# Two SSD heads in turn on the two column halves, and gate squares summed in full precision

## The reference

```python
y_diag = jnp.einsum('bgcls,bghcls,bcsghp->bclghp', cb, Lmat, xc)        # inside a chunk of 128 tokens
...
y_off = jnp.einsum('bclgn,bcghpn,bghcl->bclghp', Cc, states, jnp.exp(a_cum))   # from the chunks before
...
y = y_fwd + y_bwd + xs * d_skip.reshape(SSM_GROUPS, SSM_HEADS_PER_GROUP)[..., None]
y = y.reshape(b, S, SSM_W) * jax.nn.silu(z)
y = rms_norm(y.reshape(b, S, SSM_GROUPS, SSM_W // SSM_GROUPS),
             norm_g.reshape(SSM_GROUPS, SSM_W // SSM_GROUPS))
```

## Time and profile before

| | us |
|---|---|
| median of 3 runs (1583.84 to 1584.5) | 1584.28 |
| the profiled execution | 1584.14 |
| its span, first to last instruction | 1582.4 |
| PE busy in it | 1554.7 |
| DVE busy | 944.8 |
| ACT busy | 733.8 |

### The profile page before, as it was taken

How to read it: one execution, slowest core, us unless ns; L and a number is a source line. 1 busy time by engine, 2 the same in 40 slices (tenths; PEclk the granted TensorE clock), 3 DMA queues, 4 the chain that set the end, 5 groups by cost and what they waited for, 6 DMA issues and landing times.

```text
span 1582.4 us, 25561 instructions
## 1 busy us (share of the span) xinstructions
PE 1554.7 (98%) x9693; PEld 1395.8 (88%) x9693; DVE 944.8 (60%) x1226; ACT 733.8 (46%) x1011; POOL 35.0 (2%) x36
## 2 busy tenths in 40 slices
PE   6999999999999999999999999999999999999998
PEld 6999999998888888888889998899988998889987
DVE  5878787778666666665465554364454455435543
ACT  4476556656354544444443443434433344424431
POOL 0000000000100000000000000000000000000000
PEclk9999999999999999999999999999999999999999
DMA  8776666555566656575656655666555665666564
GB/s 233 227 216 175 184 174 174 172 175 154 161 186 175 180 176 178 175 237 180 195 181 182 185 183 192 193 166 183 190 190 171 186 181 192 191 174 183 186 196 136
DMA packets 186324, 291.50 MB, mean 184 GB/s; under 512 B 13533, under 2 KB 67151, under 8 KB 185984
## 3 DMA queue, kind: packets, MB, share of 16 engines
q1 hardware_dynamic: 183748, 285.92, 60.3%
q10 hardware_dynamic: 2492, 4.36, 0.9%
HBM read 288.04 MB, written 5.34 MB: 185 GB/s over the span
## 4 chain that ended last, share of the span: by engine, by line
PE 95%; DMA 2%; DVE 1%; ACT 1%; issue 0%; DVEq 0%; SPq 0%; ACTq 0%
PE psum L1178 94%; DMA raw<-in_w_in 1%; DVE w_lo L776 1%; DMA x_in<-in_x 1%; PE psum L1288 0%; PE psum L1308 0%; PE psum L1221 0%; DMA decay_rows<-prefix 0%; PE psum L1231 0%; ACT w_hi L478 0%; DVE xg L751 0%; ACT mix L507 0%; ACT squares_act L464 0%; DVE actT_lo L771 0%; SPq L298 0%
## 5 line engine op out<-in xcount | busy, mean ns | idle before, releaser
L776 DVE TENSOR_TENSOR w_lo<-raw,w_hi 128x1024 fp32r<-128x1024 f32 x512 | 611.0, 1221 | 165.4 <-ACT w_hi L478 162.0
L478 ACT ACTIVATE w_hi<-raw 128x1024 fp32r<-128x1024 f32 x512 | 527.8, 1053 | 390.0 <-DMA raw<-in_w_down 166.2
L1178 PE MATMUL psum<-actT_lo,w_hi 128*128 128x256 f32 x1792 | 514.1, 287 | 9.6 <-DVE w_lo L776 9.6
L1178 PE MATMUL psum<-actT_hi,w_hi 128*128 128x256 f32 x1792 | 509.5, 284 | 0.0
L1178 PE MATMUL psum<-actT_hi,w_lo 128*128 128x256 f32 x1792 | 509.4, 284 | 0.0
L1178 PEld LDWEIGHTS psum<-actT_lo,w_hi 128*128 128x128 f32 x1792 | 346.3, 193 | 14.4 <-DVE w_lo L776 9.4
L1178 PEld LDWEIGHTS psum<-actT_hi,w_lo 128*128 128x128 f32 x1792 | 346.3, 193 | 0.2
L1178 PEld LDWEIGHTS psum<-actT_hi,w_hi 128*128 128x128 f32 x1792 | 346.3, 193 | 0.0
L1178 PE MATMUL psum<-w_hi,hid_lo 128*128 128x512 f32 x512 | 199.2, 389 | 0.0
L1178 PE MATMUL psum<-w_lo,hid_hi 128*128 128x512 f32 x512 | 199.2, 389 | 0.0
L1178 PE MATMUL psum<-w_hi,hid_hi 128*128 128x512 f32 x512 | 199.2, 389 | 0.0
(11 more groups left out here) (192 smaller groups left out, 1277.7 us busy)
## 6 DMA issues: line engine op xcount, KB each, us to landing
raw<-in_w_in SPq DMA_DIRECT2D x128, 512.0 KB
raw<-in_w_up SPq DMA_DIRECT2D x128, 512.0 KB
raw<-in_w_down SPq DMA_DIRECT2D x128, 512.0 KB
raw<-in_w_out SPq DMA_DIRECT2D x64, 512.0 KB
raw<-in_w_in SPq DMA_DIRECT2D x64, 256.0 KB
raw<-in_w_in SPq DMA_DIRECT2D x128, 128.0 KB
decay<-decay_rows SPq DMA_DIRECT2D x16, 512.0 KB, 5.5
rel_tiles<-rel_rows ACTq DMA_DIRECT2D x1, 3072.0 KB, 19.8
```

What stands on the lines that cost most here:

```text
L478: act.activation(w_hi[j][:, :, :], raw[j][:, :, :], ACT.Copy).then_inc(hi_ready, 1)
L776: tt_(w_lo[j][:, :, :], raw[j][:, :, :], w_hi[j][:, :, :].bitcast(f32), ALU.subtract).then_inc(lo_dve, 1)
L1178: return pe.matmul(o, lhsT, rhs, start=first, stop=last, **kw)
```

## The change

It has three parts. The four products of two heads are issued in turn: first product of the even head, first of the odd one, then the second of each, and so on. The squares of the gate are summed as they are by fp32 matmuls with one moving column; the rounded copy, the low part, their tiles and their semaphores go. And the two loads of decay rows in a window are issued at slots 4 and 16 instead of 2 and 14.

```diff
@@ SP, decay_loads
-                if s == 2 and m is not None:
+                if s == 4 and m is not None:
                     sp.wait_ge(decays_ready, 8 * m + 4)
                     load_decay(2 * m + 1)
-                if s == 14 and m is not None and w is not None:
+                if s == 16 and m is not None and w is not None:
                     sp.wait_ge(decays_ready, 8 * w)
                     load_decay(2 * w)
@@ ACT, ssd_slot
                         act.activation(gate_sq[:, :, :], gate[:, :, :], ACT.Square).then_inc(gate_squared, 1)
-                        act.wait_ge(gate_squared, G + 1)
-                        act.activation(sq_hi[:, :, :], gate_sq[:, :, :], ACT.Copy).then_inc(sq_high, 1)
@@ DVE, ssd_slot
-                    if k == 9:
-                        dve.wait_ge(sq_high, G + 1)
-                        tt_(sq_lo[:, :, :], gate_sq[:, :, :], sq_hi[:, :, :].bitcast(f32), ALU.subtract)\
-                            .then_inc(sq_low, 1)
@@ PE, ssd_slot
                     if k in (5, 7):
                         pe.wait_ge(xtok_ready, G + 1)
                         pe.wait_ge(mix_ready, 4 * G + k - 3)
-                        for h in (k - 5, k - 4):
-                            rows, ch = slice(64 * (h % 2), 64 * (h % 2) + 64), slice(64 * h, 64 * h + 64)
-                            c0 = SEQ * (h // 2)
-                            both, second, first = slice(c0, c0 + SEQ), slice(c0 + P, c0 + SEQ), slice(c0, c0 + P)
-                            mm(M0[rows, both], xdt_f[:, 0, ch], mix[h][:, 4:6, :], True, False)
-                            mm(M0[rows, both], xdt_b[:, 1, ch], mix[h][:, 0:2, :], False, False)
-                            mm(M0[rows, second], xdt_f[:, 1, ch], mix[h][:, 2, :], False, False)
-                            mm(M0[rows, first], xdt_b[:, 0, ch], mix[h][:, 3, :], False, True).then_inc(y_done, 1)
+
+                        for n, (xdt, t, blocks, c0, c1) in enumerate((
+                                (xdt_f, 0, slice(4, 6), 0, SEQ), (xdt_b, 1, slice(0, 2), 0, SEQ),
+                                (xdt_f, 1, slice(2, 3), P, SEQ), (xdt_b, 0, slice(3, 4), 0, P))):
+                            for h in (k - 5, k - 4):
+                                base = SEQ * (h // 2)
+                                ins = mm(M0[64 * (h % 2):64 * (h % 2) + 64, base + c0:base + c1],
+                                         xdt[:, t, 64 * h:64 * h + 64], mix[h][:, blocks, :], n == 0, n == 3)
+                                if n == 3:
+                                    ins.then_inc(y_done, 1)
                     if k == 10:
-                        pe.wait_ge(sq_low, G + 1)
-                        pe.wait_ge(ones_rounded, 1)
+                        pe.wait_ge(gate_squared, G + 1)
                         pe.wait_ge(cb_masked, G + 1)
                         for t in range(TT):
-                            for n, (sq, c) in enumerate(((sq_lo, 0), (sq_lo, 1), (sq_hi, 0), (sq_hi, 1))):
-                                ins = mm(M1[:, 2 * t:2 * t + 2], sq[:, c, P * t:P * t + P], ones_r[:, 0:2], n == 0, n == 3)
+                            for c in range(2):
+                                ins = mm(M1[:, 2 * t:2 * t + 1], gate_sq[:, c, P * t:P * t + P],
+                                         ones_r[:, 0:1].bitcast(f32), c == 0, c == 1)
                         ins.then_inc(norm_summed, 1)
```

More of the change, by code:

```diff
@@ L172, in build @@
         rnorm = place("rnorm", [P, SEQ], at=at_of(lo2, 1024))
-        sq_hi = place("sq_hi", [P, 2, SEQ], f32r, at=cat_base + 32768)
-        sq_lo = place("sq_lo", [P, 2, SEQ], f32r, at=at_of(lo2, 2048))
         norm_ms, norm_root = small[:, 32:34], small[:, 34:36]
@@ L240, in build @@
         x_in_s = [sem(f"x_in{t}") for t in range(TT)]
-        table_in, ones_rounded, sq_high, sq_low = (sem(n) for n in ("table_in", "ones_rounded", "sq_high", "sq_low"))
+        table_in, ones_rounded = sem("table_in"), sem("ones_rounded")
         rows_in, relw_in, col_in, dtw_in, dskip_in = (sem(n) for n in (
```

## The result

The changed kernel takes 1568.96 us in the median (four runs, 1568.2 to 1569.55) against 1584.06 for the kernel before: a ratio of 0.9904, with a 95% interval of 0.9887 to 0.9921. The forecast was 1569.0.

What follows compares the result with a forecast made beforehand. The prediction took PE (TensorE), busy 98% of the span, as the bound. 1584.14 - 14.6 (products) - 0.7 (clock) = 1568.8, other terms zero; the median lies 0.14 above, so 1569.0 us, range 1566 to 1573.5.

Steps and rivals of the forecast that it cites:

- The products: SSD products of two heads in turn: first to last start falls from 2.16 to 1.25 us, 14.6 us over 16 pairs.
- The look ahead: SSD products in PE's queue: PE passes over three unstarted records today, so it should pass over one in the new order.
- Rival 1: SSD products: starts follow the program order, 1.51 us a pair, gain only 10.4 us, 1573.2 us; chance 0.10.
- Rival 3: SSD products: alternation serialises the halves, 2.55 us a pair against 2.16, +6.2 us, 1589.8 us; chance 0.04.
- Rival 4: SSD products: the overlap is only how records are drawn, so the order is indifferent, 1584 us; chance 0.03.
- The sums: Sums of squares of the gate: eight records a group stay eight, about 0.1 us each, so zero.
- Neither bound: Sums of squares: -3.6 us if four records only, +0.8 us if a restart of 0.1 us at each group.
- The dropped operations: One ACT copy and one DVE subtraction a group: nobody on PE waits for them, so worth nothing.
- the decay loads: Two DMAs each issued two slots later on SP: weights are fetched with lead, so zero on PE.
- the link from sums to spread: PE, GpSimd, DVE, PE between sums and spread: lead of 0.38 us remains, costed at nothing.
- Rival 2: Spread: DVE and ACT fall behind in shorter windows, a new wait gives 7.2 us back, 1576 us; chance 0.05.
- The clock: Gaps between MLP quarters: one and a half lower-clock episodes instead of two, -0.7 us, between -3.0 and +1.5.

Runs made afterwards that it cites:

- turns of two and three: The changed kernel, but each head issues two, or three, products before the other has its turn: 1569.31 and 1576.67 us (one execution each).

## Why the prediction was right, and where it wasn't

**The products: right in mechanism and size.** 0.91 us a pair and 14.6 us were forecast; PE's records give 40.96 - 26.35 = 14.6. The step that carried it was the reading of the earlier trace rows, a start of the second head ahead of the first head's last records, with neither slower. The look ahead was sized from the same rows (over three records), and turns of two and three confirmed it; that it ends there could be read in the same timeline, where B stood still with four ahead. Rivals 1, 3 and 4 fell: 1.25 us a pair, not 1.51; 2.54 only where both heads share a half; and the order is not indifferent.

**The sums: right.** Zero was taken; 7.2 us of PE's program before and after, and a ratio of 1.000 for that part alone. Neither bound was needed.

**The dropped operations and the decay loads: zero was right for each alone, wrong beside the new order.** The prediction took the longest idle of SP to be without worth, since PE did not wait for weights, and looked at the link from sums to spread in one later group only. There the stretch isn't shortened, and the 0.38 us of lead did remain. In group 0, DVE was late in the kernel before already, and the lead there, 0.70 us, was spent by the 1.8 us by which the sums came sooner. Rival 2 had the mechanism; it struck in one group, not in eight, 1.3 us with the order alone, and the decay loads, costed at nothing, kept it away. Without them, but with the other two parts, it cost 0.7 us.

**The clock: mis-sized.** -0.7 us was taken for half an episode less. Both profiled executions had two, and over all profiles 27 of 36 gaps drew one, so 2.25 would have been the better guess than 1.5, and the term about zero (without it the forecast is 1569.7). The profiled executions differ by 1584.14 - 1569.34 = 14.8 us: 14.6 for the products and 0.2 for a shorter wait for the first conv output (0.5 and 0.3 us). So nothing stands for the 0.7 in the profiles. That the median came out at 1569.0 as forecast is in part luck: the single executions lie between 1568.2 and 1569.55, and a fourth one moved the median of the kernel before from 1584.28 to 1584.06.

## What to carry to other kernels

Where a matmul's output fills half the partitions, issue it in turn with one for the other half, with no more than three records between; look in the timeline for a start that comes ahead of program order, since it shows both that halves overlap and how far PE looks. When PE is the bound and a stretch of its program shrinks, check each link PE, VectorE, GpSimd, PE in the worst group, not in a typical one, and mind what stands ahead of the link's step in each queue. And read the gaps that every iteration of an outer loop repeats: here moving one late addition gave 10.2 us, more than half of what the products gave.

## What the runs showed of the hardware

- Two fp32 streams on the two column halves run at full rate together: 0.43 us for two and two records of 256 columns, 0.87 us when all four are on one half.
- PE started records of the other half past three unstarted ones, and waited where there were four or five: B's first start came 0.01 us behind the record of A that left three, in the kernel before (109.44) and in turns of three (108.39).
- An fp32 matmul with one moving column and 128 stationary ones leaves two records 0.11 us apart, as a float32r one with two columns leaves one in 0.11: the width of the moving operand doesn't show.
- After 27 of 36 idle stretches of 2.6 to 2.7 us the granted clock fell to the lower of its levels (1.2 GHz), with matmuls in the gap after none of three, and with the gaps shortened to 0.9 us or less after none of three. Each episode costs 1.4 to 1.5 us. What decides between gaps of the same length stays open.
- The same root on GpSimd took 0.70 us in 15 of the 112 groups in all profiles and 1.6 in 97. VectorE stood idle at the start of all 15, and was in the midst of a low part of weights (1.22 us) at the start of all 97. No run varied this alone, so that the one causes the other is not shown.
